# Attention of the sample group: four stages joined into one program, with scores of four batches in PSUM

## The reference

```python
def logical(pool, new):
    rows = pool[page_table].reshape((bn, past) + pool.shape[2:])
    return jnp.concatenate([rows, new], axis=1)
kc, vc = compress_kv(logical(pool_ck, k_cmp), logical(pool_cv, v_cmp), kg_cmp)  # means of 64 rows; keys normed
ksb, vsb = to_blocks(logical(pool_sk, k_slc)), to_blocks(logical(pool_sv, v_slc))
kw, vw = concat(win_k, k_win), concat(win_v, v_win)          # window of 512
# nsa_query_block:
pc = softmax(q.kc*scale + bias)                # 32 blocks
top_idx = top_k(forced or pc.sum(heads), 16)   # blocks that stay open
ps = softmax(q.ks*scale + bias, only open blocks)
pw = softmax(q.kw*scale + bias, window)
o = gate0*(pc.vc) + gate1*(ps.vs) + gate2*(pw.vw)
```

## Time and profile before

| what | us |
|---|---|
| device time, median of 3 runs | 3174.81 (3173.14 to 3176.52) |
| device time of the profiled execution | 3171.49 |
| its span, first to last instruction | 3169.6 |
| the four sample stages, from the first bias DMA to the first DMA of the merge | 248.2 |
| of these: rows / scores / softmax / values | 17.98 / 139.92 / 23.70 / 66.60 |

### The profile page before, as it was taken

How to read it: one execution, slowest core, us unless ns; L and a number is a source line. 1 busy time by engine, 2 the same in 40 slices (tenths; PEclk the granted TensorE clock), 3 DMA queues, 4 the chain that set the end, 5 groups by cost and what they waited for, 6 DMA issues and landing times. The chain is left out here.

```text
span 3169.6 us, 49239 instructions
## 1 busy us (share of the span) xinstructions
PE 2765.9 (87%) x21538; PEld 2467.6 (78%) x21538; DVE 1193.9 (38%) x2077; ACT 783.2 (25%) x1219; POOL 153.7 (5%) x212
## 2 busy tenths in 40 slices
PE   5898688886997789947589999899887999999998
PEld 3896388864995555524479999899677999999998
DVE  5433544435144466526321333433443222222222
ACT  3222222211124334411221221211423112222211
POOL 1000122201111000011000000000000000000000
PEclk8997699987997799978789999998988999999999
DMA  4610100005420000045521111311301111111111
GB/s 164 215 48 10 16 3 3 3 4 161 112 62 3 1 1 1 1 173 190 220 63 47 44 51 46 91 53 41 113 20 34 47 47 47 47 47 40 47 47 62
DMA packets 178838, 192.10 MB, mean 61 GB/s; under 512 B 18166, under 2 KB 162793, under 8 KB 173520
## 3 DMA queue, kind: packets, MB, share of 16 engines
q1 hardware_dynamic: 168113, 126.91, 13.6%
q0 software_dynamic: 9888, 61.87, 5.5%
q10 hardware_dynamic: 624, 0.18, 0.0%
HBM read 165.28 MB, written 28.00 MB: 61 GB/s over the span
## 5 line engine op out<-in xcount | busy, mean ns | idle before, releaser
L586 PE MATMUL ps<-xf_h,ff_high 128*128 128x352 f32 x768 | 248.8, 324 | 14.0 <-DVE ff_low L575 14.0
L3179 PE MATMUL ps<-ff_hidden_high,ff_high 128*128 128x352 f32 x768 | 249.2, 325 | 4.8 <-issue 4.8
L3181 PE MATMUL ps<-ff_hidden_high,ff_low 128*128 128x352 f32 x768 | 249.0, 324 | 0.0
L3180 PE MATMUL ps<-ff_hidden_low,ff_high 128*128 128x352 f32 x768 | 249.0, 324 | 0.0
L588 PE MATMUL ps<-xf_h,ff_low 128*128 128x352 f32 x768 | 247.4, 322 | 0.0
L587 PE MATMUL ps<-xf_l,ff_high 128*128 128x352 f32 x768 | 247.2, 322 | 0.0
L2810 PE MATMUL ps<-xn_h,me_gate_w_high 128*128 128x352 f32 x576 | 186.6, 324 | 9.6 <-DVE me_gate_w_low L2868 9.6
L2811 PE MATMUL ps<-xn_l,me_gate_w_high 128*128 128x352 f32 x576 | 185.2, 322 | 0.0
L2812 PE MATMUL ps<-xn_h,me_gate_w_low 128*128 128x352 f32 x576 | 185.0, 321 | 0.0
L3223 DVE TENSOR_TENSOR x<-x,ps 128x1056 f32<-128x1056 f32 x64 | 80.3, 1254 | 236.0 <-PE ps L3181 236.0
L3217 DVE TENSOR_TENSOR ff_hidden_low<-ff_act,ff_hidden_high 128x1056 fp32r<-128x1056 f32 x32 | 40.3, 1259 | 321.6 <-ACT ff_hidden_high L3205 321.6
(11 more groups left out here) (662 smaller groups left out, 6420.2 us busy)
## 6 DMA issues: line engine op xcount, KB each, us to landing
ff_raw<-in_w_ff SPq DMA_DIRECT2D x64, 512.0 KB, 4.0
me_gate_w_raw<-in_w_in SPq DMA_DIRECT2D x24, 512.0 KB, 3.9
pj_raw<-in_w_in SPq DMA_DIRECT2D x13, 512.0 KB, 5.1
xn_high<-xn_h POOLq DMA_DIRECT2D x1, 4224.0 KB, 12.2
xn_low<-xn_l POOLq DMA_DIRECT2D x1, 4224.0 KB, 23.7
xn_h<-xn_high POOLq DMA_DIRECT2D x1, 4224.0 KB, 16.7
xn_l<-xn_low POOLq DMA_DIRECT2D x1, 4224.0 KB, 26.8
xn_h<-xn_high SPq DMA_DIRECT2D x1, 4224.0 KB, 13.0
```

The source lines that it names most:

```text
L586: e.matmul(o, W.hi[:, z, k, :], rh[:, k, n], start=k == ks[0], stop=False)
L3179: e.matmul(o, W.hi[:, u % NSPL, 2 * k + z, :], hh[:, r, ns], start=k == 0, stop=False)
L3180: e.matmul(o, W.hi[:, u % NSPL, 2 * k + z, :], hl[:, r, ns], start=False, stop=False)
L3181: mm = e.matmul(o, W.lo[:, u % NSPL, 2 * k + z, :], hh[:, r, ns], start=False, stop=k == GB - 1)
```

## The change

The four stages become one, `stage_sample_attn`, with one block and no barriers between.

- The keys and window keys of batch 0 are loaded in `stage_nsa_prompt`, into memory of their own.
- The scores of a quad stay in PSUM: bank `z` holds product `z` for 128 rows, and bank 5 the small products. DVE takes a bank out once per quad, 128 partitions at a time (`scores_out`).
- PE works ahead: it turns group `G + 5` between products, and the means of batch `b` come at product 3 of batch `b`. ACT has a ring of 8 turned groups.
- The softmax of quad 0 is spread over batches 4 to 7; that of quad 1 lies beside the values of quad 0.
- POOL's gathers keep the order of their waits; the gathers of values 0 and 1 follow the keys of batches 4 and 5. SP issues the window loads, the bias, gates, new values and the two reloads of the normed input in one queue.

```diff
@@ stage_nsa_prompt
+        @block.gpsimd
+        def _(e):
+            e.wait_ge(K.out_sem("tail_stored"), 16 * K.tail_stores)
+            gather(e, sk[:, :], K.d["cache_slc_k"], idx, 0).then_inc(K.out_sem("s_keys_near"), 16)
         @block.sync
         def _(e):
+            e.dma_start(wk[:, :, :], K.d["cache_win_k"][0, 0]...).then_inc(K.out_sem("s_window_near"), 16)
@@ stage_sample_attn, gpsimd
+            for b in range(DB):
+                if b >= 2:
+                    e.wait_ge(s_m, b - 1)
+                gather(e, ck[b % 2][:, :], K.d["cache_cmp_k"], idx, b).then_inc(s_c[b % 2], 16)
+                gather(e, cv[b % 2][:, :], K.d["cache_cmp_v"], idx, b).then_inc(s_c[b % 2], 16)
+                if b >= 2:
+                    e.wait_ge(s_t, NTG * (b - 1))
+                if b >= 1:
+                    gather(e, key(b)[:, :], K.d["cache_slc_k"], idx, b).then_inc(s_k[b % 2], 16)
+                if b in (4, 5):
+                    values(b - 4)
+            e.wait_ge(s_t, NTG * (DB - 1))
+            values(2)
+            for b in range(3, DB):
+                e.wait_ge(s_used, b - 2)
+                values(b)
@@ sync
+            window_keys(1)
             (the 8 bias DMAs, the two stores of rows)
+            window_values(0)
+            window_values(1)
+            for b in range(2, DB):
+                e.wait_ge(s_t, NTG * (b - 1))
+                window_keys(b)
+                if b == 2: (wait for the stores; 8 loads of grow, 2 of vnew)
+            e.wait_ge(s_m, DB)
+            again(0)
+            for b in range(2, DB):
+                if b == 4:
+                    e.wait_ge(s_t, NTURN)
+                    e.wait_ge(s_ev, 12)
+                    again(1)
+                e.wait_ge(s_used, b - 1)
+                window_values(b)
@@ tensor
+            def turn(G):
+                b, z = G // NTG, G % NTG
+                if z == 0:
+                    keys_landed(e, b)
+                if z == 4:
+                    window_landed(e, b)
+                if G >= 2:
+                    e.wait_ge(s_tc, G - 1)
+                (four transposes to bank 6 + G % 2) .then_inc(s_t, 1)
+            def means(b):
+                e.wait_ge(s_slot, 2 * b + 2)
+                ...
+            for G in range(LEAD):
+                turn(G)
+            e.wait_ge(s_qb, 1)
+            for G in range(NTURN):
+                b, z = G // NTG, G % NTG
+                if z == 0 and b >= 1:
+                    head_sums(b - 1)
+                if z == 2 and b >= 1:
+                    new_scores(b - 1)
+                    if b == 6:
+                        block_scores(0)
+                if G + LEAD < NTURN:
+                    turn(G + LEAD)
+                score(G)
+                if z == 3:
+                    means(b)
+            head_sums(DB - 1)
+            new_scores(DB - 1)
+            e.wait_ge(s_ex, 3)
+            (turn the probabilities of quad 0)
+            block_scores(1)
+            (wait for their copies; values(0); turn those of quad 1; turned_out(0); values(1); turned_out(1))
@@ scalar, after the first five copies
+            for G in range(NTURN):
+                b, z = G // NTG, G % NTG
+                if G + LEAD < NTURN:
+                    copy(G + LEAD)
+                if z == 0 and b >= 1:
+                    root(b - 1)
+                if (b, z) == (5, 1):
+                    exps(0, 0)
+                    exps(0, 1)
+                if (b, z) == (7, 1):
+                    exps(0, 2)
+            root(DB - 1)
+            probs_out(0)
+            (exps(1, n) for n in 0, 1, 2; probs_out(1))
@@ vector
+            slot_sum(0, 0)
+            slot_sum(0, 1)
+            e.wait_ge(s_b, 16 * 2 * DT)
+            (copy of the bias for blocks)
+            for b in range(DB):
+                (b == 4: new_scores_out(0), side_max(0); b == 5: block_probs(0); b == 6: top_blocks(0))
+                if b % 4 == 3:
+                    scores_out(q, 0), scores_out(q, 1), scores_out(q, 2)
+                means_out(b)
+                if b % 4 == 3:
+                    scores_out(q, 3)
+                if b + 1 < DB:
+                    slot_sum(b + 1, 0)
+                if b % 4 == 3:
+                    scores_out(q, 4)
+                if b == 6:
+                    shut_blocks(0)
+                mean_square(b)
+                if b + 1 < DB:
+                    slot_sum(b + 1, 1)
+                block_keys(b)
+            (new_scores_out(1) to weights(1); combine and to_channels of both quads)
```

More of the change, by code:

```diff
@@ L2376, with gather @@
 SROW = SS + SWN + SCM
[L2379 to L2383, removed]
+SLOTS = PAST // P
+def gather(e, dst, cache, idx, b):
+    rows = cache[0].rearrange("g (e s) h d -> (g e) (s h d)", s=SLOTS)
+    return e.indirect_dma_start(dst, None, rows, bass.IndirectOffsetOnAxis(ap=idx[:, b:b + 1], axis=0))
@@ L2385, in _, with window_keys, window_values, again @@
         @block.sync
         def _(e):
+            def window_keys(b):
+                e.dma_start(win(b)[:, :, :], K.d["cache_win_k"][0, b].rearrange("(i p) g d -> p i (g d)", p=P)).then_inc(s_wk[b % 2], 16)
+            def window_values(b):
+                e.dma_start(wv[:, b % 2, :, :], K.d["cache_win_v"][0, b].rearrange("(i p) g d -> p i (g d)", p=P)).then_inc(s_wv[b % 2], 16)
+            def again(z):
+                dst, src = moves[z]
+                e.dma_start(dst.bitcast(F32), src.bitcast(F32)).then_inc(K.out_sem("xn_again"), 16)
@@ L2398, in _ @@
             e.dma_start(K.gscr[:, 768:KVG], gates[:, :]).then_inc(s_g, 16)
[L2399 to L2420, removed]
@@ L2423 @@
-SLOTS = PAST // P
-def gather(e, dst, cache, idx, b):
-    rows = cache[0].rearrange("g (e s) h d -> (g e) (s h d)", s=SLOTS)
-    return e.indirect_dma_start(dst, None, rows, bass.IndirectOffsetOnAxis(ap=idx[:, b:b + 1], axis=0))
[L2432 to L2467, removed]
@@ L2471, in _ @@
             ident, blk = K.c("ident"), K.c("blk16")
+            rows = lambda b: slice(32 * (b % 4), 32 * (b % 4) + 32)
+            def turn(G):
[6 more added lines that the diff above has]
+                    e.wait_ge(s_tc, G - 1)
+                for j in range(4):
+                    src = slot(key(b), 4 * z + j) if z < 4 else win(b)[:, j, :]
+                    mm = e.transpose(K.ps[:, 6 + G % 2, P * j:P * j + P], src, ident)
+                mm.then_inc(s_t, 1)
@@ L2484, in _ @@
[L2484 to L2497, removed]
-                    for j in range(4):
[L2499 to L2520, removed]
@@ new lines, in values @@
+            def values(q):
+                for b in range(4 * q, 4 * q + 4):
+                    e.wait_ge(s_pgs[b % 3], 16 * (b // 3 + 1))
+                    e.wait_ge(s_wv[b % 2], 16 * (b // 2 + 1))
+                    r = rows(b)
+                    for j in range(SLOTS):
+                        e.matmul(K.ps[r, 2, 0:P], PT[:, j, r], slot(sv[b % 3], j), start=j == 0, stop=False)
+                    e.matmul(K.ps[r, 2, 0:P], PN[0:DT, 0, r], vnew[0:DT, b, 0, :], start=False, stop=True)
+                    for j in range(4):
+                        e.matmul(K.ps[r, 3, 0:P], PT[:, NPG + j, r], wv[:, b % 2, j, :], start=j == 0, stop=False)
+                    e.matmul(K.ps[r, 3, 0:P], PN[0:DT, 1, r], vnew[0:DT, b, 1, :], start=False, stop=True)
+                    e.matmul(K.ps[r, 4, 0:P], PN[:, 2, r], vcb[:, b, :], start=True, stop=True).then_inc(s_used, 1)
@@ new lines, in _ @@
+            head_sums(DB - 1)
+            new_scores(DB - 1)
+            e.wait_ge(s_ex, 3)
+            e.wait_ge(s_tc, NTURN)
+            for z in range(6):
+                probs(0, z)
+            e.wait_ge(s_ev, 12)
+            block_scores(1)
+            e.wait_ge(s_ptc, 6)
+            e.wait_ge(s_r, 16 * (2 * DT + 2))
+            values(0)
+            e.wait_ge(s_ex, 6)
+            for z in range(6):
+                probs(1, z)
+            turned_out(0)
+            e.wait_ge(s_ptc, 12)
@@ L2522, in _, with copy @@
+            values(1)
+            turned_out(1)
         @block.scalar
         def _(e):
[L2524 to L2530, removed]
-                    e.activation(KT[:, lo:lo + 512], K.ps[:, G % 2, :], ACT.Copy).then_inc(s_tc, 1)
-                    if z == 3:
-                        e.wait_ge(s_v, b + 1)
-                        e.activation(rt[:, :], rt[:, :], ACT.Sqrt).then_inc(s_r, 1)
+            def copy(G):
+                e.wait_ge(s_t, G + 1)
+                if G >= RING:
+                    e.wait_ge(s_s, G - RING + 1)
+                e.activation(KT[:, G % RING, :], K.ps[:, 6 + G % 2, :], ACT.Copy).then_inc(s_tc, 1)
@@ new lines, in root, with exps, probs_out @@
+            def root(b):
+                e.wait_ge(s_v, b + 1)
+                e.activation(rt[:, :], rt[:, :], ACT.Sqrt).then_inc(s_r2, 1)
+            def exps(q, n):
+                z = (2, 1, 0)[n]
+                lo, hi = RNG[z]
+                e.wait_ge(s_mx, 3 * q + n + 1)
```

(33 more changed lines are left out.)

365 lines of the change are left out of this document (197 added, 168 removed).

## The result

| what | before | after |
|---|---|---|
| device time, median of 4 runs | 3173.97 us (3170.16 to 3176.52) | 3198.11 us (3196.60 to 3199.75) |
| ratio to before, 95% interval | | 1.0077 [1.0060, 1.0095] |
| span of the profiled execution | 3169.6 | 3196.9 |
| mean granted clock of TensorE | 0.917 | 0.912 |
| start of the merge in the span | 1614.31 | 1635.85 |

The forecast was 3208 (3180 to 3226). The difference of the medians is 24 us, under 1%, and the interval of the ratio lies clear of 1. Of the 27.3 us by which the profiled span is longer, 21.5 lie ahead of the merge, where the change is, and 5.8 behind it.

A forecast was written before the change was run, and what follows sets the result against it. PE would wait for keys in every batch: means(0) at 1408.0, six batches of 25.5 us (153.0) and a tail of 86 put the merge at 1647.0, +32.7 on the median 3174.81, forecast as 3208 us (3180 to 3226).

The forecast's parts named there:

- The loop has no slack, so a batch costs L + W: Batch loop: waiting for keys and PE's work follow in series, 25.5 us a batch (23.8 to 27.5) against 15.7.
- L: Batch loop: time from the end of the means to the next keys landed, 13.2 us (12.0 to 13.8).
- W: Batch loop: time from key(b) landed to the end of means(b-1), 12.3 us (11.8 to 13.7).
- Rival A: Batch loop: keys don't hold PE, a batch is PE's own 12.5 us; -45, 3130 us; chance 0.10.
- The start: Stage start: first product waits for key(1), landing at 1396.1 with bias delay; means(0) end at 1408.0 (1394.3 to 1409.4).
- Rival C: Stage start: the bias doesn't hold key(1); -13, so 3195 us; included in the forecast's chance of 0.80.
- Rival E: Stage start: keys loaded ahead save nothing, as turn(5) wants key(1); part of the forecast, no chance of its own.
- four turns and products 4 x 1.97: Term of W: PE's four turns and products after the keys land, 7.9 us at full clock.
- rival D: Batch loop: PE's clock never recovers in W; +50 more, 3258 us; chance 0.04.
- The tail: From the end of means(6) to the merge: 86 us (82 to 89).
- `window_values(4)`, queued behind it, has 30 us: Tail: window values queued behind the second reload of the normed input have 30 us; the reloads lie under the values.

The follow-up runs named there:

- e1: Changed kernel with the gather of keys issued ahead of the wait for the means, from batch 2 on; 3131.11 us, ratio to before 0.9867.
- e2: Changed kernel with the keys gathered first of the three gathers, still behind the wait for the means; 3164.92 us, ratio to before 0.9959.
- e4: Changed kernel with the bias loads issued only after the first turn of batch 1; 3191.33 us, ratio to before 1.0053.
- e7: Changed kernel with each bias DMA filling 32 adjacent partitions, outermost size 8 instead of 4, same bytes; 3193.64 us, ratio to before 1.0057.
- e6: e5 plus the bias shape of e7 and the block choice of quad 0 behind the block keys of batch 6; 3096.62 us, ratio to before 0.9747.
- e5: Changed kernel with e1 (for batch 1 too), e3 and e4 together; 3123.36 us, ratio to before 0.9838.
- e3: Changed kernel with the second reload of the normed input behind the last window values in SP's queue; 3187.84 us, ratio to before 1.0041.
- e9: Changed kernel with 30 evictions of 32 partitions added to DVE, their results overwritten; 3202.27 us, ratio to before 1.0087.

## Why the prediction was right, and where it was not

**The mechanism.** The step "The loop has no slack, so a batch costs L + W" held: the two windows above show it, and e1 and e2 took it away in two parts. Rival A's price (3130) was met by e1 at 3131, which is what the change would have given had the keys not held PE; that it was met so closely is luck, as six batches took 66.7 us there and not 75, and the tail 92.0 and not 86.

**The start.** Key(1) forecast at 1396.1, seen at 1397.8; end of means(0) 1408.0, seen 1408.5. The mechanism held, but the closeness is luck. The five gathers were taken as 16.6 us and took 19.8 without the bias (e4). The bias was taken as 13 us and cost 10.8; the 13 has no row behind it either, since 0.33 MB an engine at the rate of the prediction's own gathers (6.8 MB in 20.5 us over 16 engines) is 16 us. And from key(1) to the end of the means it is 10.7 us, not 11.9. Rival C (the bias doesn't hold key(1)) fell by e4 and e7. The Trainium skill, "DMA: Bandwidth & Descriptors", section "Why a DMA increments its semaphore by 16 and not by 1", says that a DMA runs on the largest number of engines up to 16 that divides the outermost sizes of its access patterns. e7 agrees: with 8 in place of 4 the same bytes held the keys 5.0 us less, and e6 lost the wait of 14.8 us that e5 had. It is no proof, as e7 also fills adjacent partitions in place of every fourth. Rival E held as it was told: the early load saves nothing that the times can show.

**L, a size off.** 13.2 forecast (12.0 to 13.8), 11.85 seen (the mean of six, 11.4 to 12.9, from the end of the means to the first turn). It took 8.1 us from issue to landing at an issue 4.82 us behind `ss_ck`; here the keys are issued 2.7 us behind ck and wait 8.6, so the issue did help, by 1.6 us net.

**W, a term mis-sized.** 12.3 forecast (11.8 to 13.7), 10.55 seen (10.0 to 11.2), so all six lie under its range. The failed term is "four turns and products 4 x 1.97": the row read as a turn of 1.07 us was one of eight instructions, which is two turns. A turn is four transposes of one instruction each, and with its product it takes 1.56 us at full clock (1448.82 to the start of the means at 1450.38 in the timeline above). 4 x 1.56 + 0.4 + 2.0 + 2.0 for the clock is 10.6. By the same error rival A's batch was put at 12.5, where e1 shows 11.1. The clock's part was about right: after each idle time PE is granted 0.50 for a while and then nearly all, as these two windows of the changed kernel show.

```profile
1441.40:1447.20 5.80, 5.78 (x18) 2.02 (x18) 0.60 (x2) 1.31 (x3) 0.00 (x0) 0.50 0.01 3
1447.20:1452.40 5.20, 5.20 (x30) 2.95 (x29) 0.00 (x0) 1.20 (x2) 0.00 (x0) 0.98 0.00 0
```

In this batch half of 5.8 us is lost, 2.9; in the batch before, with 0.82 over 10.25 us, it is 1.8. Over the six it comes to 1.9 (10.55 less 4 x 1.56 + 0.4 + 2.0), where 2.0 was taken; rival D (no recovery) is out. A batch is so 22.4 us (134.40 / 6) and not 25.5, below its range of 23.8 to 27.5, and six of them make the forecast 18.6 us too long, 8.1 by L and 10.5 by W.

**The tail, a wrong step.** Forecast 86 from the end of means(6), seen 1635.85 - 1542.90 = 92.95. The step that failed is "`window_values(4)`, queued behind it, has 30 us": it was costed at nothing and cost 8.7, by e3 10. The buffer that these values go to is free only when batch 2 has been worked off, so the issue comes 9.4 us ahead of the use. Without it the tail is 84.2, within 82 to 89. The wait for DVE at batch 6 that the prediction named is there (6.0 us); e6 cut it to 1.5, and 3.5 came up at the next head sum.

**What the forecast had not.** From the start of the merge to the end the changed kernel takes 1561.05 us, before 1555.3, with the same code. In the memory stage, 790 us behind the start of the merge, the kernel before and the changed one, in this order:

```profile
2404.31:2429.31 25.00, 24.22 (x138) 24.22 (x139) 4.26 (x4) 4.59 (x5) 0.00 (x0) 0.89 0.23 64
```

```profile
2425.85:2450.85 25.00, 18.78 (x102) 18.78 (x103) 6.07 (x4) 7.16 (x7) 0.00 (x0) 0.77 0.17 43
```

The clock granted is 0.89 in the one and 0.77 in the other. The ten runs of the experiments, which have this code too, show 1554.4 to 1561.4 us for the same piece (e9 1554.4, e5 1557.4, e1 1561.1). So the 5.8 us are no more than what this piece varies by between programs with the same code there; what decides it is open. Ten of the eleven programs with the joined stage lie at 1557.4 or above, though, so with one trace of the kernel before it isn't shown either that the change has no part in it.

**The sum again.** +0.5 at the start, -18.6 in the batches, +7.0 in the tail: 1647.0 becomes 1635.9, +21.5 against before where +32.7 was forecast. With the 5.8 behind it the profiled execution is +27.3; the medians differ by 24.1. So the sign and the serial loop were forecast rightly, but that the time came within 10 us is partly luck: the batches and the tail both left their ranges, in opposite directions, and the piece behind the merge, which the sum had at nothing, made up for some more.

## What to carry to other kernels

When a program is made to work a step ahead, go through every wait that lets a load out and every queue that it stands in: a release left at its old place while its use moves forward turns a hidden transfer into a serial one, here 10 us a batch. Work taken from an engine is worth what the path gives for it: the same 30 evictions, in the same place of DVE's order, cost 4 us while PE stood for the keys and 37 once it did not. And count the instructions of a row (x8 is not x4) before its time is taken for a step.

## What the runs showed of the hardware

A small load can delay large gathers by more than its bytes: 1.31 MB of bias at a DMA share of 0.26 held 5.2 MB of gathers, which took 19.8 us without it (e4), by 10.8 us (9 to 11 by the other traces with this start); the same bytes in e7's shape held them by 5.0 us less (3 to 6). A gather of 1.05 MB was there 5.7 to 8.0 us after its issue (median 6.0, e2) at the head of a burst of three, and 8.4 to 9.9 as the third (changed kernel). And a piece of some 1555 us with unchanged code varied by up to 7 us between programs, with a granted clock of 0.77 or 0.89 in the same 25 us of it.
